# Expert weights loaded in pairs of chunks, 16 KB in one piece to a partition, with the transposes' steps to match

## What is computed

```python
def expert_block(args):
    xblk, e = args
    hu = jnp.dot(xblk, w_up[e]) + b_up[e]
    g = jnp.minimum(hu[:, 0::2], SWIGLU_LIMIT)
    u = jnp.clip(hu[:, 1::2], -SWIGLU_LIMIT, SWIGLU_LIMIT)
    act = (u + 1.0) * g * jax.nn.sigmoid(SWIGLU_ALPHA * g)
    return jnp.dot(act, w_down[e]) + b_down[e]
```

## Time and profile before

| | us |
|---|---|
| median of three runs | 1650.87 |
| lowest, highest | 1649.14, 1663.30 |
| the profiled execution | 1654.17 |
| its span, first to last instruction | 1652.4 |

### The profile page before, as it was taken

One profiled execution on the slowest core, in us unless ns is written; L12 is line 12 of the kernel. 1 busy time (PEld: TensorE's weight loads), 2 busy tenths in 40 slices (PEclk: granted clock), 3 DMA queues, 4 the chain that ended last, 5 costly groups with the idle time before them and its releaser, 6 DMA issues.

```text
span 1652.4 us, 21727 instructions
## 1 busy us (share of the span) xinstructions
PE 1402.2 (85%) x6257; PEld 997.2 (60%) x6258; DVE 1239.3 (75%) x1254; ACT 939.2 (57%) x864; POOL 295.6 (18%) x416
## 2 busy tenths in 40 slices
PE   5993586989988999999899999999988998999660
PEld 3762465654537667666676666667766766767440
DVE  0245564755548999999889999999988898898745
ACT  0011323602116877887678878877767776787522
POOL 5302989820300001000100101001000000000000
PEclk8997787659898999999999999999999999999885
DMA  9975364052418999999989999999988999899734
GB/s 350 364 246 155 91 209 170 1 152 81 161 37 320 384 405 395 393 407 398 367 318 404 395 401 389 393 406 398 397 314 335 383 407 369 325 403 406 260 129 150
DMA packets 124955, 498.52 MB, mean 302 GB/s; under 512 B 21106, under 2 KB 46275, under 8 KB 91027
## 3 DMA queue, kind: packets, MB, share of 16 engines
q1 hardware_dynamic: 104146, 454.56, 71.6%
q0 software_dynamic: 14768, 29.16, 5.2%
q10 hardware_dynamic: 5984, 14.11, 2.4%
HBM read 499.43 MB, written 26.25 MB: 318 GB/s over the span
## 4 chain that ended last, share of the span: by engine, by line
PE 42%; DVE 25%; issue 15%; ACT 8%; SPq 6%; DMA 3%; DVEq 1%; ACTq 0%; POOL 0%; POOLq 0%
PE psum L537 39%; DVE w_lo L1789 14%; SPq L391 4%; ACT w_hi L1243 4%; PE psum L540 3%; ACT arena L1203 2%; DMA early<-in_pages 1%; DVE arena L1812 1%; DMA arena<-y_dram 1%; DVE arena L1814 1%; DVE x_split L1844 1%; DVE arena L1433 1%; DVE arena L1434 1%; DVE arena L1335 1%; DMA arena<-in_w_down 1%
## 5 line engine op out<-in xcount | busy, mean ns | idle before, releaser
L1789 DVE TENSOR_TENSOR w_lo<-arena,w_hi 128x2048 fp32r<-128x2048 f32 x352 | 795.4, 2287 | 107.9 <-ACT w_hi L1243 107.3
L1243 ACT ACTIVATE w_hi<-arena 128x2048 fp32r<-128x2048 f32 x344 | 652.9, 1913 | 238.1 <-PE psum L537 233.9
L537 PE MATMUL psum<-arena 128*128 128x64 f32 (+10 forms) x2194 | 464.9, 385 | 41.0 <-DMA arena<-in_w_in 18.7
L537 PE MATMUL psum<-w_hi,x_split 128*128 128x512 f32 x1628 | 441.0, 399 | 14.8 <-DVE x_split L1844 6.0
L537 PE MATMUL psum<-w_lo,x_split 128*128 128x512 f32 x1408 | 401.5, 407 | 58.8 <-DVE w_lo L1789 53.9
L537 PEld LDWEIGHTS psum<-arena 128*128 128x128 f32 (+3 forms) x2194 | 300.4, 194 | 205.6 <-issue 157.7
L537 PEld LDWEIGHTS psum<-w_lo,x_split 128*128 128x128 f32 x1408 | 255.1, 190 | 171.6 <-DVE w_lo L1789 124.8
L537 PEld LDWEIGHTS psum<-w_hi,x_split 128*128 128x128 f32 x1628 | 305.7, 191 | 79.6 <-issue 12.5
L2003 POOL DMA_INDIRECT y_dram<-y_part,arena x32 | 38.4, 1199 | 1004.2 <-DVE y_part L1850 731.0
L540 PE MATMUL psum<-arena 128*128 128x128 f32 (+4 forms) x581 | 96.2, 320 | 84.3 <-ACT arena L1087 30.0
L540 PEld LDWEIGHTS psum<-arena 128*128 128x128 f32 (+4 forms) x581 | 79.2, 167 | 103.6 <-issue 42.5
(11 more groups left out here) (229 smaller groups left out, 750.7 us busy)
## 6 DMA issues: line engine op xcount, KB each, us to landing
arena<-in_w_up SPq DMA_DIRECT2D x256, 1024.0 KB, 7.6
arena<-in_w_down SPq DMA_DIRECT2D x128, 1024.0 KB, 7.2
early<-in_pages SPq DMA_DIRECT2D x160, 128.0 KB, 2.7
arena<-in_w_in ACTq DMA_DIRECT2D x23, 512.0 KB, 7.3
arena<-in_pages POOLq DMA_DIRECT2D x32, 128.0 KB, 7.0
early<-in_pages POOLq DMA_DIRECT2D x32, 128.0 KB, 6.4
arena<-in_pages SPq DMA_DIRECT2D x32, 128.0 KB, 2.2
early<-in_w_plg SPq DMA_DIRECT2D x1, 4096.0 KB, 14.5
```

Source lines behind the costliest of these rows:

```text
L537: return TE.matmul(out, lhsT, rhs, start=start, stop=stop, skip_group_check=True)
L1243: SE.activation(w_hi[:, (8 + t) % 3], chunk_in[(8 + t) % 6], ACT.Copy).then_inc(hi_ready, 1)
L1789: VE.tensor_tensor(w_lo[:, at], chunk_in[buf], w_hi[:, at].bitcast(f32), SUB).then_inc(lo_ready, 1)
```

## The change

Two neighbouring chunks are now one transfer of 2 MB, so there are three pair buffers (`pair_in`) over the same six chunks, and three `w_here` semaphores. The chunks are still copied, subtracted and multiplied one by one. The fifth and sixth chunk buffers must be neighbours, so the sixth moves by 256 columns. So that a pair is 16 KB in one piece to a partition, partition p holds other rows of the weights than before: two neighbouring rows of w_up in a pair, four neighbouring rows of w_down. The transposes pick the columns of x and of the hidden rows to match: x with a step of 2 elements, the hidden rows with a step of 8. A pair's load waits until both chunks of its buffer are done with. In the prologue the pair of chunks 4 and 5 waits for the last product of the gate (`("plg", 2, 1)`), where only chunk 5 did.

```diff
-        chunk_in = [arena[:, k * SLOT:(k + 1) * SLOT] for k in range(4)] + [arena[:, R0:R0 + SLOT], arena[:, M0:M0 + SLOT]]
-        assert SLOT <= KT * NT and SLOT == 2 * D
+        chunk_in = [arena[:, k * SLOT:(k + 1) * SLOT] for k in range(4)] + [arena[:, R0:R0 + SLOT], arena[:, R0 + SLOT:R0 + 2 * SLOT]]
+        pair_in = [arena[:, 0:2 * SLOT], arena[:, 2 * SLOT:4 * SLOT], arena[:, R0:R0 + 2 * SLOT]]
...
-            up = A["w_up"].rearrange("e (k p) n -> e k p n", p=128)
-            down = A["w_down"].rearrange("e (k a p) n -> e k p a n", p=128, a=2)
+            up = A["w_up"].rearrange("e (k p a) n -> e k p (a n)", p=128, a=2)
+            down = A["w_down"].rearrange("e (k p a) n -> e k p (a n)", p=128, a=4)
...
-                sp.dma_start(dst, src).then_inc(w_here[buf], 16)
+                of, k = (up, c // 2) if c < 8 else (down, (c - 8) // 2)
+                src = of[e, k] if isinstance(e, int) else of[bass.ds(e, 1), k].rearrange("e p n -> (e p) n")
+                sp.dma_start(pair_in[buf // 2], src).then_inc(w_here[buf // 2], 16)
...
+            full(sp, ("plg", 2, 1))
             weights(0, 4)
-            full(sp, ("plg", 2, 1))
-            weights(0, 5)
...
-                if t == (3 if last else 11):
-                    sp.wait_ge(chunk_used, i * PER + (8 + t + 1 + 3))
+                if t == (2 if last else 10):
+                    sp.wait_ge(chunk_used, i * PER + (8 + t + 2 + 3))
                 else:
-                    sp.wait_ge(lo_ready, i * SPLIT + (8 + t + 1))
+                    sp.wait_ge(lo_ready, i * SPLIT + (8 + t + 2))
...
             def item_loads(i, e):
-                for t in range(PER):
+                for t in range(0, PER, 2):
...
-                    last = turn(psum[:, 6 + k // 4, (k % 4) * CAP:(k % 4 + 1) * CAP], xg[:, k * 128:k * 128 + 128])
+                    last = turn(psum[:, 6 + k // 4, (k % 4) * CAP:(k % 4 + 1) * CAP], xg[:, 256 * (k // 2) + k % 2:256 * (k // 2) + k % 2 + 255:2])
...
+            def hidden_columns(s, j):
+
+                first = 1024 * (j // 4) + 2 * (j % 4) + s
+                return hu[:, first:first + 8 * 127 + 1:8]
...
-                            cols = hu[:, 2 * j * 128 + s:2 * (j + 1) * 128:2]
-                            last = mm(psum[:, 6 + s, j * HALF:(j + 1) * HALF], cols, folder, True, True)
+                            last = mm(psum[:, 6 + s, j * HALF:(j + 1) * HALF], hidden_columns(s, j), folder, True, True)
...
-                act.wait_ge(w_here[buf], s // 6 * 16 + 16)
+                act.wait_ge(w_here[buf // 2], s // 6 * 16 + 16)
...
-        b_up=a["b_up"][0].reshape(NE, 8, 128, 2).transpose(2, 0, 3, 1).reshape(128, NE, 16),
+        b_up=a["b_up"][0].reshape(NE, 2, 128, 4, 2).transpose(2, 0, 4, 1, 3).reshape(128, NE, 16),
```

More of the change, by code:

```diff
@@ L299, in build @@
         entries = ec.take(3, TOPK, ENTRY).bitcast(i32)
-        chunk_in = [arena[:, k * SLOT:(k + 1) * SLOT] for k in range(4)] + [arena[:, R0:R0 + SLOT], arena[:, M0:M0 + SLOT]]
-        assert SLOT <= KT * NT and SLOT == 2 * D
+        chunk_in = [arena[:, k * SLOT:(k + 1) * SLOT] for k in range(4)] + [arena[:, R0:R0 + SLOT], arena[:, R0 + SLOT:R0 + 2 * SLOT]]
+        pair_in = [arena[:, 0:2 * SLOT], arena[:, 2 * SLOT:4 * SLOT], arena[:, R0:R0 + 2 * SLOT]]
+        assert R0 + 2 * SLOT <= X0 and SLOT == 2 * D
         many_i = page_ids
@@ L333, in build @@
         mask_ready, G_ready, items_ready, rank_ready = sem("mask_ready"), sem("G_ready"), sem("items_ready"), sem("rank_ready")
-        w_here, hi_ready, lo_ready, chunk_used = many("w_here", 6), sem("hi_ready"), sem("lo_ready"), sem("chunk_used")
+        w_here, hi_ready, lo_ready, chunk_used = many("w_here", 3), sem("hi_ready"), sem("lo_ready"), sem("chunk_used")
         act_hi_ready, act_lo_ready = sem("act_hi_ready"), sem("act_lo_ready")
@@ L473, in _ @@
             full(sp, ("wo", 2, 1))
-            for c in range(4):
+            for c in (0, 2):
                 weights(0, c)
@@ L478, in _ @@
                 sp.dma_start(h_dram[m * 128:m * 128 + MT[m]], h[0:MT[m], m]).then_inc(h_stored, 16)
+            full(sp, ("plg", 2, 1))
             weights(0, 4)
-            full(sp, ("plg", 2, 1))
-            weights(0, 5)
             def next_weights(i, t, e, c, buf, last=False):
-                if t == (3 if last else 11):
-                    sp.wait_ge(chunk_used, i * PER + (8 + t + 1 + 3))
+                if t == (2 if last else 10):
+                    sp.wait_ge(chunk_used, i * PER + (8 + t + 2 + 3))
                 else:
-                    sp.wait_ge(lo_ready, i * SPLIT + (8 + t + 1))
+                    sp.wait_ge(lo_ready, i * SPLIT + (8 + t + 2))
                 weights_to(e, c, buf)
             def first_loads(r):
-                for t in range(8):
+                for t in (0, 2, 4, 6):
                     e, c = (0, t + 6) if t < 2 else (1, t - 2)
@@ L502, in last_loads @@
             def last_loads(i):
-                for t in range(6):
+                for t in (0, 2, 4):
                     of, c = (NE - 1, t + 6) if t < 2 else (NE - 2, t + 6)
                     next_weights(i, t, of, c, (8 + t) % 6)
-                for t in range(6, 10):
+                for t in (6, 8):
                     next_weights(i, t, NE - 1, t + 2, (8 + t) % 6)
@@ L520, in _ @@
                 with sp.If(n_items > r * NE):
-                    for c in range(6):
+                    for c in (0, 2, 4):
                         i, t = (r * NE - 2, 10 + c) if c < 2 else (r * NE - 1, c - 2)
@@ L916, in turn_hidden @@
                         for j in range(8):
-                            last = turn(psum[:, to + j // 4, (j % 4) * CAP:(j % 4 + 1) * CAP], hu[:, 2 * j * 128 + s:2 * (j + 1) * 128:2])
+                            last = turn(psum[:, to + j // 4, (j % 4) * CAP:(j % 4 + 1) * CAP], hidden_columns(s, j))
                         last.then_inc(hu_turned, 1)
@@ L971, in product @@
                         last.then_inc(chunk_used, 1)
-                    pe.wait_ge(w_here[buf], i * 32 + ((first + 3) // 6 * 16 + 16))
+                    pe.wait_ge(w_here[buf // 2], i * 32 + ((first + 3) // 6 * 16 + 16))
                     for a, c in ((0, 0), (0, 1), (1, 0), (1, 1)):
@@ L1240, in part @@
                 def part(t):
-                    act.wait_ge(w_here[(8 + t) % 6], i * 32 + ((8 + t) // 6 * 16 + 16))
+                    act.wait_ge(w_here[(8 + t) % 6 // 2], i * 32 + ((8 + t) // 6 * 16 + 16))
                     act.wait_ge(chunk_used, s + (t + 1))
```

5 lines of the change are left out of this document (removed).

## The result

The changed kernel takes 1815.19 us (median of four, 1812.48 to 1818.03), the kernel before 1654.39 beside it. The ratio is 1.097, with a 95% interval of 1.091 to 1.102: 9.7% slower, some 160 us, where 3% was forecast. The sign was right and the size wrong by a factor of three.

The account below looks back on a forecast made before the run. The engines' chain, mostly TensorE and VectorE, was taken to bound the kernel, not DMA. Quiet items 33.3, seven others 10.5, long items 3.2, three more 4.5 and prologue 0.5 made 52 us on 1650.9: 1703 us, range 1662 to 1728.

Parts of the forecast that it names:

- The bound: Whole kernel before: path runs through the engines, DMA 3% of it; faster loads can return only 3.9 us.
- Faster by 1% or more: Rival, 4%: items paced by DMA, longer pieces move 440 in place of 400 GB/s, up to 2 us an item, 1600 us.
- Fewer issues on SP: Six DMA issues an item go away on SP, which is not on the path: 0.
- The step of 8: Transposes of hidden rows in the fold on TensorE: 50 ns a weight load, 1.6 us an item, bounds 0 and 2.75.
- the four long items: Items with many slots, 38.5 to 42.3 us: 16 transposes at 50 ns, 0.8 us each item, 3.2 together.
- The clock: Granted clock in quiet items: expected to stay 1.00, with no cost in the sum; falling below would make the forecast wrong.
- The step of 2 for x: Transposes of x: eight weight loads take 1.03 us as when contiguous, so 0.
- The loads: Pairs alone: later release and landing cost 0.85 us a quiet item (0 to 1.7); as pairs-only rival 19 us, 1670, 25%.
- the two landing times: A 2 MB pair lands 7.5 us after issue when alone, or 4.9 us after the pair ahead of it.
- That the two don't add up: Quiet item: step shifts work by 1.45 us and gives loads room, pairs add 0.4, together 1.85.
- the forecast's own 18, 7 and 3: Items in its sum: 18 quiet at 1.85 us, 7 of 33.5 us at 1.5, 3 outside the 29 periods at 1.5.
- dear case: Rival, 7%: stride at VectorE's price, 2.75 us a fold, +2.8 an item, 81 us in all, 1732 us.

Follow-up runs that it names:

- the probe: The changed kernel with spaced pairs of loads, then matmuls and transposes at chosen steps, after its last output; only those stretches count, some 300 us longer was expected.
- steps_only: The changed kernel's rows and transpose steps, with the 1 MB loads and six buffers of the kernel before: 1798.83 us, 1.085 of the kernel before.
- pairs_old_steps: The changed kernel's 2 MB pairs in three buffers, with the rows and steps of the kernel before: 1744.64 us, 1.051 of the kernel before.

## Why the prediction was wrong

**The bound** was read rightly: before, no load was on the path, so the pairs had nothing to win. Faster by 1% or more had 4%. That rival's price was loosely worked: 440 in place of 400 GB/s would be 9% of an item of 32.34 us, 2.9 us and not 2. Nothing hangs on it, since no load was late.

**Fewer issues on SP**: nothing on the path, as said.

**The step of 8 was the worst sized term.** It was put at 1.6 us an item, bounded by 2.75 from VectorE's reduction. It is 3.84 us for the fold (7.69 against 3.85). The failed step is "128 columns at 2.4 GHz are 53 ns of it, which a halved read would double": the probe shows the whole 120 ns of a fold step doubling. The upper bound failed too, for it took the price in ns from another engine's row, where 86 ns was on 286, and not its own step as the thing that could double. The Trainium skill (SBUF — State Buffer, Door 1: The DMA port swizzle, the note on cachelines) says that a 16-byte line wants two hits; the probe's 0.12, 0.17 and 0.23 us at steps 2, 3 and 4 agree for the fp32 matmul. By that rule the transposes would pay too, and their row shows no price at step 8. The forecast charged them 3.2 us in the four long items; in steps_only those four together are 1.5 us longer than before.

**The clock had no term.** It stood only among the things that would make the forecast wrong. It falls within the fold, and the first chunk behind it takes 2.8 us of weight loads in place of 1.6: 1.1 to 1.4 us an item, on the path. Fold and clock together are 3.85 + 1.2 = 5.05 us; steps_only shows 37.5 - 32.3 = 5.2. The fold itself is not slower by the clock: its 32 loads start 0.24 us apart before and after the fall. A fold at a step of 2 is another matter. In the kernel before, one runs at 1.2 GHz:

```profile
518.18 6.90 PEld L537 LDWEIGHTS psum<-arena 128*128 128x128 f32 x32 [2.96 <-issue]
...
518.20:525.10 6.90, 6.90 (x33) 6.90 (x33) 6.37 (x3) 4.09 (x3) 0.00 (x0) 0.50 0.71 267
```

It takes 6.90 us where it takes 3.85 at 2.4 GHz. So doubled time alone would not tell a slow clock from a slow read; the first half of the changed kernel's fold, at 2.4 GHz, does.

**The step of 2 for x** is not quite 0: eight loads take 1.15 us (668.17 and 818.98 us in the changed kernel) where they took 1.03. The reading of the earlier trace rows missed it: the two groups are equally long, but a load of the hidden columns at 817.40 takes 209 ns, one of x 141. The 0.12 us stands beside other waits.

**The loads.** The estimate of 6.8 us for a pair was low against 7.5 to 7.8; the fit that it came from stands in the Trainium skill (DMA: Bandwidth & Descriptors, Anatomy of one DMA) for loads issued by GpSimd, and these are issued by SP. The places of the waits (chunks 0, 2 and 8) and the two landing times, 7.5 and 4.9, hold. Mis-sized is what came on top: 0.9 us an item was allowed. Over 51 loads of pairs_old_steps between 880 and 1180 us the landing was on average 0.59 us later than the two rules say, 3.5 us for the six loads of an item. The 16 that were issued 2 to 4 us before the load ahead of them landed carry 19 of the 30 us; they fall on other pairs from item to item, and 8-9 is late by most (1.3 us on average). The probe has the same case alone with 1.4 to 1.9 us. How much of the rest is gather and scatter was not taken apart. So the pairs cost 84 us where the sum said 19.

**That the two don't add up** was right in kind: 139 us for the steps and 84 for the pairs make 161 together, so on top of the steps the pairs add 22. ACT's waits for weights in the whole kernel are 156 us in the changed kernel and 191 in pairs_old_steps; that the others stand beside the longer fold and cost nothing there is argued, not shown.

**Sum with the measured terms**: (3.84 + 1.2) of the steps, less 0.15 of slack, is 4.9 an item. The fold runs in the 28 items that aren't long (the forecast's own 18, 7 and 3), and 28 x 4.9 = 137, where steps_only shows 139. The forecast had 1.45 in the place of 4.9. The pairs' 22 us on top are 0.8 an item, where it had 0.4. The range ended at 1728, just under its dear case of 1732, and that one used the same VectorE row.

## What to carry to other kernels

When an edit changes the step of an operand, take the whole instruction as what may double, and count how many elements share 16 bytes. Where the writer can scatter, try it there and let the reader read in order: here that cost ACT 0.2 us an item and saved TensorE 3.85. When a stretch of matmuls gets slower by waiting for its weights, give the clock a term, for the stretch and for what follows it. Halving the number of buffers by doubling their size makes every first half wait for its second and frees every first half late. Here no load was late before, so there was nothing to win, and it cost 84 us; whether it pays with more memory, as many buffers of the double size, was not tried.

## What was unexpected of the hardware

- The weights of an fp32 matmul read at a step of 4 elements or more take 0.23 to 0.27 us for 128 columns against 0.12 at a step of 1 or 2; eight transposes take 1.07 us at a step of 8 and 1.03 at 1 (but 1.15 at 2).
- A fold step with slow reads takes the same 0.24 us at 2.4 and at 1.2 GHz (starts 0.24 us apart on both sides of the fall), while the fold at a step of 2 goes from 3.85 to 6.90 us: the slow read doesn't follow the clock, the fast one does.
- The granted clock fell to 1.2 GHz in a stretch in which PE was busy all the time with matmuls of 64 columns behind slow weight loads, and right behind such a stretch when it was no longer than before (3.89 us against 3.85, where 32 loads in place of 16 kept 2.4 GHz).
- A 2 MB load issued 2.6 to 3.0 us before the one ahead of it comes in lands 1.4 to 1.9 us later than its own 7.5 us and the 4.9 behind the other would give; one issued 3.8 or 1.8 us before it does not.
